# Attention head groups of two layers in the order main, difference, difference, sparse, with the index key rotated on VectorE

## The reference

```python
for l in range(DEPTH):                       # DEPTH = 2
    h = rms_norm(x, attn_norm_g[l])
    proj = h @ w_in[l]
    (mq, mk, mv, dq, dk, dv, sq, sk, sv, iq, ik, iw) = jnp.split(proj, offsets, axis=-1)
    moba = moba_attention(qk(mq, 4, qg[0]), qk(mk, 4, kg[0]), split_heads(mv, 4))       # "main"
    diff = diff_attention(dq_h[:, 0::2], dq_h[:, 1::2], dk_h[:, 0::2], dk_h[:, 1::2], dv4, lam)
    diff = rms_norm(diff, diff_subln_g[l]) * (1.0 - lam_init)
    dsa = dsa_attention(sq4, sk4, sv4, apply_rope(iq, 8 heads), apply_rope(ik),         # "sparse"
                        iw * (IDX_HEADS ** -0.5))
    mix = jnp.concatenate([moba, diff, dsa], axis=-1)       # 256 + 512 + 256 columns
    x = x + mix @ w_out[l]
    h2 = rms_norm(x, ffn_norm_g[l])
    x = x + (silu(h2 @ w_gate[l]) * (h2 @ w_up[l])) @ w_down[l]
```

## Time and profile before

| | |
|---|---|
| median of 3 runs | 1314.15 us (1314.12 to 1315.04) |
| the profiled execution | 1313.64 us, span 1311.8 us |
| mean granted TensorE clock | 0.979 |
| TensorE busy | 1265.5 us, 96% of the span |
| VectorE, ScalarE, POOL busy | 821.8, 664.2, 196.6 us |
| mixer of layer 0 and of layer 1, from the second input product | 24.85 to 170.84 and 370.30 to 515.31 us |

### The profile page before, as it was taken

One profiled execution on the slowest core, in us unless ns is written; L12 is line 12 of the kernel. 1 busy time (PEld: TensorE's weight loads), 2 busy tenths in 40 slices (PEclk: granted clock), 3 DMA queues, 4 the chain that ended last, 5 costly groups with the idle time before them and its releaser, 6 DMA issues.

```text
span 1311.8 us, 16910 instructions
## 1 busy us (share of the span) xinstructions
PE 1265.5 (96%) x6430; PEld 1067.9 (81%) x6430; DVE 821.8 (63%) x975; ACT 664.2 (51%) x981; POOL 196.6 (15%) x186
## 2 busy tenths in 40 slices
PE   8997999999999979999999999999999999999998
PEld 6776888888887868888888899788998777788886
DVE  6897365555569945555556765776686677744454
ACT  5566354444465644544445454565455744544443
POOL 5884100000276711000000000000000003000000
PEclk9999799999999969999999998999999999999999
DMA  7344046555462332555555463423324455455551
GB/s 256 141 152 166 33 152 216 183 189 207 152 215 87 127 129 97 212 182 185 189 188 200 149 247 137 161 79 142 129 97 175 146 193 184 169 208 190 181 201 51
DMA packets 34218, 213.11 MB, mean 162 GB/s; under 512 B 4305, under 2 KB 5585, under 8 KB 11506
## 3 DMA queue, kind: packets, MB, share of 16 engines
q1 hardware_dynamic: 34098, 212.21, 45.4%
q0 software_dynamic: 64, 0.13, 0.0%
HBM read 211.28 MB, written 1.05 MB: 162 GB/s over the span
## 4 chain that ended last, share of the span: by engine, by line
PE 73%; DVE 13%; issue 4%; POOL 4%; ACT 4%; DMA 2%; SPq 0%; POOLq 0%; DVEq 0%; ACTq 0%
PE bank L598 20%; PE bank L600 20%; PE bank L599 20%; DVE wlo L1689 4%; PE bank L1007 3%; PE bank L764 2%; PE bank L705 2%; DVE index L1769 2%; ACT whi L1233 1%; PE bank L724 1%; PE bank L852 1%; PE bank L626 1%; DMA raw<-in_w_out 1%; ACT probs L1310 1%; DVE index L1788 1%
## 5 line engine op out<-in xcount | busy, mean ns | idle before, releaser
L1689 DVE TENSOR_TENSOR wlo<-raw,whi 128x2048 fp32r<-128x2048 f32 (+3 forms) x197 | 444.3, 2262 | 253.7 <-ACT whi L1233 252.7
L1233 ACT ACTIVATE whi<-raw 128x2048 fp32r<-128x2048 f32 (+5 forms) x201 | 369.2, 1843 | 160.7 <-PE bank L600 149.7
L598 PE MATMUL bank<-whi,hT_hi 128*128 128x512 f32 (+4 forms) x1040 | 406.5, 391 | 8.8 <-DVE wlo L1689 5.2
L600 PE MATMUL bank<-whi,hT_lo 128*128 128x512 f32 (+4 forms) x1040 | 398.4, 383 | 0.0
L599 PE MATMUL bank<-wlo,hT_hi 128*128 128x512 f32 (+4 forms) x1040 | 397.8, 383 | 0.0
L598 PEld LDWEIGHTS bank<-whi,hT_hi 128*128 128x128 f32 x1040 | 196.6, 189 | 48.0 <-DVE wlo L1689 8.9
L600 PEld LDWEIGHTS bank<-whi,hT_lo 128*128 128x128 f32 x1040 | 196.4, 189 | 36.4
L599 PEld LDWEIGHTS bank<-wlo,hT_hi 128*128 128x128 f32 x1040 | 196.8, 189 | 33.1
L598 PE MATMUL bank<-whi,mixT_hi 128*128 128x512 f32 (+1 forms) x248 | 96.1, 387 | 3.7 <-DVE mixT_lo L1724 1.6
L600 PE MATMUL bank<-whi,mixT_lo 128*128 128x512 f32 (+1 forms) x248 | 93.7, 378 | 0.0
L598 PE MATMUL bank<-whi,ffT_hi 128*128 128x512 f32 x240 | 93.7, 390 | 0.0
(11 more groups left out here) (282 smaller groups left out, 1532.2 us busy)
## 6 DMA issues: line engine op xcount, KB each, us to landing
raw<-in_ff_loop SPq DMA_DIRECT2D x90, 1024.0 KB, 4.8
raw<-in_w_groups SPq DMA_DIRECT2D x64, 1024.0 KB, 4.8
raw<-in_w_out SPq DMA_DIRECT2D x8, 1024.0 KB, 5.4
raw<-in_ff_first SPq DMA_DIRECT2D x6, 1024.0 KB, 4.9
raw<-in_w_values SPq DMA_DIRECT2D x8, 728.0 KB, 4.1
raw<-in_w_comp SPq DMA_DIRECT2D x4, 1024.0 KB, 6.4
raw<-in_ff_last SPq DMA_DIRECT2D x3, 1024.0 KB, 6.7
raw<-in_w_values SPq DMA_DIRECT2D x4, 736.0 KB, 6.6
```

What stands on the lines that cost most here:

```text
L598: eng.matmul(out, lhsT=hi, rhs=wh, start=start, stop=False)
L600: return eng.matmul(out, lhsT=lo, rhs=wh, start=False, stop=stop)
L1233: eng.activation(whi[j][:, 0:n], raw[j][:, 0:n], ACT.Copy).then_inc(hi_ready, 1)
L1689: eng.tensor_tensor(wlo[j][:, 0:n], raw[j][:, 0:n], whi[j][:, 0:n].bitcast(F32), ALU.subtract).then_inc(lo_ready, 1)
```

## The change

Two layers' mixers are put in another order; the feed-forward parts and the third layer are as they were.

- The groups come in the order main, difference, difference, sparse (before: difference, difference, main, sparse), so the products do too: the main heads' product is number 2, ahead of the two difference products, and the main values and first difference values come earlier. The columns of `z` and the weights on the host are laid out for it; `w_out` is cut and put together in the same order of rows as before.
- The index key leaves POOL: `index_key` makes it on VectorE with four instructions behind `lambda_value`, counted by a semaphore of its own, `key_ready`. `prep` counts 5 a layer, not 6. The factor of the index weights moves into `index_relu`'s scale.
- On TensorE the products and the groups are interleaved anew. `mix_turn(0, r)` turns the first half of `mix` (main and first difference group) ahead of `group_turn(2)` and of the sparse heads' turns. The quarters of `out_product` start ahead of `group_turn(3)`. The second half is turned behind the four quarters of the first, directly ahead of `out_product(0, 1, 0)`.
- ScalarE's and VectorE's lists follow. Ahead of the second half's copies (`turned_hi_copy`, `turned_lo_copy`) now stand `split_hi(t0, FFN1)` and `split_lo(t0, FFN1)`.
- Waits are added for what is shared in the new order: `blend` for `o_done`, the sparse `turn_heads` for `turned_lo`, `mix_turn` for `heads_copied`, `out_product(1, 0, r)` for both copies of the last group, and `group_values` for its own value product.

```diff
-                        eng.wait_ge(prep, l * 6 + 6)
+                        eng.wait_ge(prep, l * 5 + 5)
...
-                eng.wait_ge(prep, l * 6 + 1)
-                for r in range(RT):
-                    projected(1, r)
-                    src = z[:, r, IK:IK + HD].rearrange("p (n d) -> p n d", d=HD)
-                    rotate(src, [rope_c[:, r, :]], [rope_s[:, r, :]], 1)
...
                     if j == 0 and n == 1:
-                        eng.wait_ge(pT_act, 2 * A + 8 + r + 1)
+                        eng.wait_ge(pT_act, 2 * A + 10)
+                        eng.wait_ge(pT_dve, A + 5)
...
+                    if s == 5:
+                        eng.wait_ge(turned_lo, l * 12 + 4 + b + 1)
...
+                def mix_turn(h, r):
+
+                    eng.wait_ge(heads_copied[r], turned_sets(l, 5 if h else 4, r) + 1)
+                    turn_part(l * 3 + 1, h, r)
...
-                index_scores(l, 0); index_scores(l, 1); index_scores(l, 2); index_scores(l, 3)
-                index_scores(l, 4); index_scores(l, 5); row_product(3, 0, 1); row_product(3, 1, 0)
-                row_product(3, 1, 1); turn_heads(2, 0); turn_heads(2, 1); row_product(4, 0, 0)
+                index_scores(l, 0); index_scores(l, 1); row_product(3, 0, 1); row_product(3, 1, 0)
+                row_product(3, 1, 1); index_scores(l, 2); index_scores(l, 3); index_scores(l, 4)
+                index_scores(l, 5); turn_heads(2, 0); turn_heads(2, 1); row_product(4, 0, 0)
                 row_product(4, 0, 1); row_product(4, 1, 0); row_product(4, 1, 1); row_product(5, 0, 0)
...
+                group_scores(0); turn_heads(3, 0); turn_heads(3, 1); row_product(5, 0, 1); row_product(5, 1, 0)
+                row_product(5, 1, 1); row_product(6, 0, 0); turn_heads(4, 0); group_turn(0); turn_heads(4, 1)
+                row_product(6, 0, 1); group_scores(1); group_values(0); row_product(6, 1, 0)
+                row_product(6, 1, 1); row_product(7, 0, 0); group_turn(1); row_product(7, 0, 1); group_values(1)
+                group_scores(2); row_product(7, 1, 0); row_product(7, 1, 1); mix_turn(0, 0); mix_turn(0, 1)
+                group_turn(2); turn_heads(5, 0); turn_heads(5, 1); group_values(2); group_scores(3)
+                out_product(0, 0, 0); out_product(0, 0, 1); group_turn(3); out_product(1, 0, 0); group_values(3)
+                out_product(1, 0, 1); mix_turn(1, 0); mix_turn(1, 1); out_product(0, 1, 0); out_product(0, 1, 1)
+                turn_part(l * 3 + 2, 0, 0); out_product(1, 1, 0); turn_part(l * 3 + 2, 0, 1)
                 out_product(1, 1, 1)
...
+                copy_z(l, 3, 0); square_heads(l, 1, 0); hi(5, 0); index_relu(l, 2); index_relu(l, 3)
+                index_relu(l, 4); copy_z(l, 3, 1); square_heads(l, 1, 1); index_relu(l, 5); heads_copy(l, 2, 0)
+                scale_heads(l, 1); heads_copy(l, 2, 1); hi(5, 1); copy_z(l, 4, 0); square_heads(l, 2, 0)
...
+                attend_exp(A + 1, 1); copy_z(l, 6, 0); square_heads(l, 3, 0); copy_z(l, 6, 1)
+                square_heads(l, 3, 1); split_hi(t0, 17); blend_copy(A + 1); scale_heads(l, 3); split_hi(t0, 18)
+                diff_stats(l, 1); copy_z(l, 7, 0); attend_exp(A + 2, 0)
+                turned_hi_copy(l * 3 + 1, mixT, halves=(0,)); split_hi(t0, 19); copy_z(l, 7, 1)
+                blend_copy(A + 2); heads_copy(l, 5, 0); heads_copy(l, 5, 1); diff_stats(l, 2)
+                attend_exp(A + 3, 1, in_bank=False); split_hi(t0, 20); attend_copy(A + 3, 0)
+                attend_copy(A + 3, 1); split_hi(t0, FFN1); turned_hi_copy(l * 3 + 1, mixT, halves=(1,))
...
+                dve(eng.tensor_tensor(turned_key[:, :, 0:h], key[:, :, h:HD], rope_s[:, :, 0:h], ALU.mult))
+                dve(eng.tensor_tensor(turned_key[:, :, h:HD], key[:, :, 0:h], rope_s[:, :, h:HD], ALU.mult))
+                dve.wait(eng)
+                dve(eng.tensor_tensor(key, key, rope_c[:, :, :], ALU.mult))
+                dve.wait(eng)
+                eng.tensor_tensor(sqr[:, 0:2 * P].rearrange("p (r a d) -> p r a d", r=RT, a=2),
...
+                head_sums(l, 2, 0); topk_rounds(2, 4); head_sums(l, 2, 1); attend_mask(A + 0, causal); lo(6, 0)
+                topk_rounds(4, 8); attend_copy(A + 0); topk_mask(); lo(6, 1); attend_mask(A + 1, causal)
+                attend_out(A + 0, 0, take(0)); lo(7, 0); blend(A + 1, 1); head_sums(l, 3, 0); head_sums(l, 3, 1)
+                blend_copy(A + 1); lo(7, 1); split_lo(t0, 17); attend_mask(A + 2, causal, (0,)); diff_norm(l, 1)
+                mixed(1); attend_mask(A + 2, causal, (1, 2)); blend(A + 2, 0)
+                turned_lo_copy(l * 3 + 1, mixT, halves=(0,)); blend_copy(A + 2); lo_from_pool(2 * l + 1)
+                split_lo(t0, 19); attend_mask(A + 3, chosen); diff_norm(l, 2); attend_copy(A + 3)
+                attend_out(A + 3, 1, take(3)); mixed(3); lo_from_pool(2 * l + 2); split_lo(t0, FFN1)
+                turned_lo_copy(l * 3 + 1, mixT, halves=(1,)); add_out(0, 0); add_out(0, 1)
```

More of the change, by code:

```diff
@@ L944, in group_turn @@
                 def group_turn(g):
-                    if g < 2:
-                        blend_turn(A + g, 2 * l + g)
+                    if g in DIFF_GROUPS:
+                        blend_turn(A + g, 2 * l + DIFF_GROUPS.index(g))
                     else:
@@ L975, in _ @@
-                turn_heads(4, 1); row_product(7, 0, 0); row_product(7, 0, 1); row_product(7, 1, 0)
-                row_product(7, 1, 1); group_turn(1); turn_heads(5, 0); turn_heads(5, 1); group_scores(2)
-                group_values(1); group_turn(2); group_scores(3); group_values(2); turn_part(l * 3 + 1, 0, 0)
-                turn_part(l * 3 + 1, 0, 1); group_turn(3); out_product(0, 0, 0); group_values(3)
-                out_product(0, 0, 1); turn_part(l * 3 + 1, 1, 0); turn_part(l * 3 + 1, 1, 1)
@@ L1418, in _ @@
-                blend_copy(A + 0); heads_copy(l, 4, 0); copy_z(l, 6, 1); square_heads(l, 3, 1); diff_stats(l, 0)
-                scale_heads(l, 3); heads_copy(l, 4, 1); attend_exp(A + 1, 1); split_hi(t0, 17); copy_z(l, 7, 0)
-                copy_z(l, 7, 1); blend_copy(A + 1); heads_copy(l, 5, 0); heads_copy(l, 5, 1); split_hi(t0, 18)
-                split_hi(t0, 19); diff_stats(l, 1); attend_exp(A + 2, 0); attend_copy(A + 2, 0)
-                attend_copy(A + 2, 1); attend_exp(A + 3, 1, in_bank=False)
@@ L1423, in _ @@
-                turned_hi_copy(l * 3 + 1, mixT, halves=(0,)); attend_copy(A + 3, 0); attend_copy(A + 3, 1)
-                split_hi(t0, 20); turned_hi_copy(l * 3 + 1, mixT, halves=(1,)); split_hi(t0, FFN1)
+                copy_z(l, 1, 0); copy_z(l, 1, 1); hi(3, 0); hi(3, 1); copy_z(l, 2, 0); square_heads(l, 0, 0)
+                heads_copy(l, 0, 0); heads_copy(l, 0, 1); copy_z(l, 2, 1); square_heads(l, 0, 1)
+                heads_copy(l, 1, 0); hi(4, 0); index_relu(l, 0); index_relu(l, 1); scale_heads(l, 0); hi(4, 1)
@@ L2024, in _ @@
-                attend_mask(A + 0, causal); lo(6, 1); blend(A + 0, 0); lo(7, 0); lo(7, 1); blend_copy(A + 0)
-                head_sums(l, 3, 0); topk_rounds(6, 8); topk_mask(); head_sums(l, 3, 1)
-                attend_mask(A + 1, causal); diff_norm(l, 0); blend(A + 1, 1); split_lo(t0, 17)
-                blend_copy(A + 1); attend_mask(A + 2, causal); diff_norm(l, 1)
-                lo_from_pool(2 * l + 1); split_lo(t0, 19); attend_copy(A + 2); attend_mask(A + 3, chosen); attend_out(A + 2, 0, take(0))
@@ L2029, in _ @@
-                mixed(2); turned_lo_copy(l * 3 + 1, mixT, halves=(0,)); attend_copy(A + 3)
-                attend_out(A + 3, 1, take(768)); mixed(3)
-                turned_lo_copy(l * 3 + 1, mixT, halves=(1,)); lo_from_pool(2 * l + 2); split_lo(t0, FFN1); add_out(0, 0); add_out(0, 1)
+                lo(1, 0); lo(1, 1); lambda_sums(l); lo(2, 0); lo(2, 1); lambda_value(l); index_key(l); lo(3, 0)
+                lo(3, 1); head_sums(l, 0, 0); head_sums(l, 0, 1); lo(4, 0); index_sum(l, 0); index_sum(l, 1)
@@ L2508, in layout @@
     t["next_first"] = np.stack([t["w1_groups"][1, 0], halves(kv)[0]])
-    t["w1_out"] = np.stack([halves(g) for g in i["w_out"]])
+    m_rows, d0_rows, d1_rows, s_rows = np.split(i["w_out"], 4, axis=1)
+    t["w1_out"] = np.stack([halves(g) for g in np.concatenate([m_rows, d0_rows, d1_rows, s_rows], 1)])
     ff = [ffn_layout(i["w_gate"][l], i["w_up"][l], i["w_down"][l]) for l in range(LAYERS)]
```

102 lines of the change are left out of this document (46 added, 56 removed).

## The result

The changed kernel takes 1323.32 us (median of 4 runs, 1321.61 to 1326.28) against 1314.13 us for the kernel before measured beside it: ratio 1.0072, 95% interval 1.0051 to 1.0093. It is slower by 9.2 us, or 0.7%. The value on record was 1317, the range 1303 to 1324, and slower had the largest chance of the three, 0.40; the case called the forecast ended at 1322. The profiled execution took 1321.61 us, the fastest of the four; its span is 1319.6 us (1311.8 before).

A forecast was written before the change was run, and what follows sets the result against it. TensorE, busy 96% of the span, was taken as the bound, so only idle time and clock count. Layers -4.5 and -4.1 give -8.6 us, clock falls +11.6: 1316.6, with 0.5 back 1317 us; range 1303 to 1324.

The forecast's parts named there:

- the case called the forecast: Clock falls in both mixers' tails, with up to two second falls: 1313 to 1322 us, chance 0.42.
- the sum: Whole kernel: 1313.64 - 8.6 + 11.6 = 1316.6 us, with 0.5 back 1317.
- A: End of row_product(6, 1, 1), cutting each layer's mixer in two; forecast 4.7 us later in layer 0, 5.9 in layer 1.
- The moved work: Ahead of A: second scores, main's values, main's transposes for the difference group's, and turn_heads(4, 1); together 6.1 us.
- the removed waits: Ahead of A: TensorE waits taken away, 3.6 us in layer 0 (index key included) and 2.4 in layer 1.
- new waits, 2.2: Ahead of A on TensorE: index_scores(5) 0.3, row_product(6, 0, 0) 0.9, turn_heads(4, 0) 1.0; bounds 0 and 5 us each layer.
- rival 2: Ahead of A: VectorE and POOL hold each other, 3.7 us a layer more plus a second fall; 1327 us, chance 0.12.
- The chain of chunk 19: Behind A: POOL's rotation, DMA at A + 12.5, ScalarE's split, then copies; group_values(2) not before A + 22.8.
- The stall that the kernel before doesn't have: Ahead of out_product(0, 1, 0): copies stand behind chunk 21's split and low part, 4.5 us.
- the fixed price a fall: Behind A: clock fall slows group 2's values, sparse scores and first out quarters; 5.8 us a layer, bounds 4 and 8.
- Rival 1: Behind A: transposes keep the clock at 2.4 GHz, saving all 11.6 us; 1305.5 us (1301 to 1309), chance 0.23.
- Rivals 3 and 4: Third: no 4.5 us stall, 1308, chance 0.10. Fourth: chunk 19's DMA sets the tail before and after, 1314.

The follow-up runs named there:

- no_contention: Changed kernel; POOL's rotation of the first difference set waits for the index sums' end and omits its table multiplications (result not the layer's); 1315.91 us, ratio 1.0019.
- low18: Changed kernel with the low part of chunk 18 made by VectorE, behind blend_copy(A + 2), instead of by POOL; 1327.5 us, ratio 1.0119.
- gain_last_before: Kernel before with SP's queue turned: loads of chunks 19 and 20 ahead of the wait for POOL's last rotation and the norm gain; 1311.84 us, ratio 0.9979.
- gain_last_after: Changed kernel with SP's queue turned: loads of chunks 19 and 20 don't wait for POOL's last rotation; 1317.54 us, ratio 1.0019.
- filler: Changed kernel with 20 and 15 matmuls to unread banks in two TensorE waits, ahead of group 2's blend and of out_product(0, 1, 0); 1317.28 us, ratio 1.0027.
- before_filler: Kernel before with 18 matmuls to an unread bank behind group_values(1), ahead of the wait for the main group's exponentials; 1307.04 us, ratio 0.9945.

## Why the prediction was right, and where it wasn't

*How near, and how much of it luck.* Against the sum the profiled execution is 5.0 us late (1321.6 for 1316.6). Up to A the two layers lost 6.5 us more than forecast; from A to the end of the mixer they took 63.35 and 68.17 us for 67.2 each (61.4 and 5.8 of clock), 2.9 less; 1.7 came behind the second mixer. The direction was right, and so were most of the waits. That the value lies within the range is in part luck: the tail of layer 0 didn't pay 4.4 us of clock, and that made up for much of what went wrong ahead of A.

*Up to A: the direction was right, the size was not.* The forecast was +4.7 and +5.9 us, the measurement +8.4 and +8.7. By the prediction's own sign (A more than 2 us off) it was wrong here. The moved work and the removed waits came as in the sum (no wait for the key, none for a rotation). Two steps failed. The first is the term "new waits, 2.2": `index_scores(5)` and `turn_heads(4, 0)` don't wait at all, but `row_product(6, 0, 0)` waits 3.1 and 2.9 us instead of 0.9. I took the six late index sums at 0.49 us, since POOL had been idle there; in the new order POOL's next rotation lies beside them and they take 0.95. The row with the 0.95 stood in the prediction as the upper bound and as rival 2. I gave the lower price because "the same engines leave 2.4 to 3.6 now", which says nothing about who runs beside whom. `no_contention` shows it (3.08 us for 5.70), and it bears out the section of the Trainium skill cited there (GPSIMD Engine Reference, Specifications). The second is a term that the sum didn't have: a clock fall behind that wait. For layer 0, 6.1 - 3.6 + 3.3 + 2.4 = 8.2, and for layer 1, 6.1 - 2.4 + 2.9 + 1.6 = 8.2.

*The chain of chunk 19.* The end of POOL's rotation is at A + 13.4 (12.5 forecast) and `group_values(2)` at A + 23.7 and 24.0 (22.8). Timelines of SP's queue, of ScalarE and of TensorE, layer 0, answering:

```profile
121.87 0.91 SPq L361 DMA_DIRECT2D raw<-in_w_out  x2
```

```profile
128.57 1.91 ACT L1230 ACTIVATE whi<-raw 128x2048 fp32r<-128x2048 f32 x1 [4.92 <-DMA raw<-in_w_out]
```

```profile
131.78 1.58 PE L739 MATMUL bank<-z,probsT 128*128 128x128 f32 x12 [1.39 <-ACT z L1256]
```

The place was right, but I hadn't seen how close the second bound lay: the blend, held 2.8 us by POOL's split of chunk 18. I had only masks, exponentials and the blend's own work in it.

*The rest.* Behind `group_values(2)` the forecast was 38.6 us. It is 39.7 in layer 0 and 44.2 in layer 1; less their clock losses (1.35 and 5.7, below) it is 38.3 and 38.5. The stall that the kernel before doesn't have was forecast at 4.5 us and measured 4.2, for the reason given: ScalarE's split and VectorE's low part of chunk 21 ahead of the copies.

```profile
153.10 1.91 ACT L1230 ACTIVATE whi<-raw 128x2048 fp32r<-128x2048 f32 x1 [8.80 <-PE bank L589]
```

```profile
155.04 2.29 DVE L1687 TENSOR_TENSOR wlo<-raw,whi 128x2048 fp32r<-128x2048 f32 x1 [3.83 <-ACT whi L1230]
157.25 1.28 DVE L1722 TENSOR_TENSOR mixT_lo<-bank,mixT_hi 128x512 fp32r<-128x512 f32 x2
```

Wait for `probsT`: 2.1 forecast, 1.9 measured.

*The clock: the right sum at the wrong places.* I put 5.8 us a layer on one fall ahead of `group_values(2)`. In layer 0 that fall came and went before the values and cost nothing; the fall in the 4.2 us stall, which I had left in the range, cost 1.35 (6.95 us for the 5.6 of two quarters). In layer 1 two falls cost something: one took the scores, 4.21 for 2.34 (+1.9), and the quarters behind them, 6.7 for 5.6 (+1.1), and one the two quarters behind the stall, 8.35 for 5.6 (+2.75). The scores of layer 1, and in both layers the quarters behind the stall up to the turn that follows them (TensorE's timeline):

```profile
158.08 0.77 PE L587 MATMUL bank<-whi,mixT_hi 128*128 128x512 f32 x1 [4.21 <-DVE mixT_lo L1722]
...
165.03 0.60 PE L615 MATMUL bank<-ident,mix 128*128 128x128 f32 x4
...
478.86 4.21 PE L694 MATMUL bank<-headsT 64*128 64x128 f32 x16
...
506.62 0.77 PE L587 MATMUL bank<-whi,mixT_hi 128*128 128x512 f32 x1 [4.21 <-DVE mixT_lo L1722]
...
514.97 0.60 PE L615 MATMUL bank<-ident,mix 128*128 128x128 f32 x4
```

That is 7.1 behind A and 4.0 ahead of it, 11.1 against the 11.6 of the forecast. The step that failed is the fixed price a fall. The work that meets the low clock takes up to twice its time, and a fall cost from nothing to 3.0 us here; which work meets it depends on where in the order the idle time ends. In layer 0 of `low18` a wait of 3.06 us ahead of `row_product(6, 0, 0)` cost next to no clock (the quarter took 3.09 us), while 3.11 cost 2.4 in the changed kernel.

*The rivals.* Rival 2 had the right mechanism (at 1327, chance 0.12, it was too dear and too unlikely); what happened is the forecast with half of rival 2 in it. Rival 1, the clock up throughout, didn't come, and it would have given less than I said: with the clock held up behind A the changed kernel takes 1317.3, not 1305.5. Of these 11.8 us, 3.7 and 2.8 are what A came too late in the two layers; the rest I haven't split up. Rivals 3 and 4 are out: the stall is there, and `gain_last_before` shows that chunk 19 didn't set the old tail.

*What the change is worth.* As it stands, it loses 9.2 us. Most of what it loses is in the order of the queues around it and not in the order of the heads: with five edits of queue order and placement it takes 1290.0 us, 25.4 below the kernel before beside it, while the three made on the kernel before gave 6.1. The two sets aren't the same edits, so this shows that the new order can be better, not by how much.

## What to carry to other kernels

When work moves to where another engine runs beside it, price it by the row with that neighbour, and ask after the move which instruction of POOL lies beside which of VectorE. After a reordering look at what stands in each queue directly ahead of the copy that TensorE waits for: a weight split for a later stage in that place cost 3.1 us and a clock fall here, twice. Where two waits end close together, try the edits together, since each alone may only lay bare the other, or move the idle time in front of dearer work.

## What the runs showed of the hardware

- A VectorE instruction of four columns took 3.00 us beside a POOL tensor_tensor of 2048 columns (4.50 us), 1.25 us beside one of 512 columns in the kernel before, and 0.22 us alone. In both kernels and both layers it had begun later than POOL's and ended within 0.02 us of it (125.94 and 125.93 us in the changed kernel, layer 0). So a long POOL instruction can hold even a tiny VectorE instruction until it ends itself.
- The granted clock fell to 1.2 GHz behind waits of 2.89 and 3.11 us (the changed kernel, ahead of A) and behind one of 1.93 (`gain_last_after`). It didn't fall behind the same wait of 2.89 in layer 1 of `filler`, nor behind one of 3.06 in `low18`, and it stayed up behind waits of 1.07 us in this tail. In `before_filler` it fell where TensorE did transposes between gaps of 0.9 to 1.2 us. So the length of the last wait alone doesn't decide it; what does isn't settled by these runs.
